# One-core hybrid decoder trunk on Trainium2: retention's weight differences on VectorE, the second norm in token layout, and GpSimd holding two groups of tiles

## The reference

```python
z = rmsnorm(h, norm_mix)
u, q, k, v, g, gate_a, gate_b = split(z @ w_in)
y_a = s5_branch(u, ...)                      # diagonal state space, GELU, GLU
y_b = retention_branch(q, k, v, g)           # 4 heads, chunks of 128, rotary, norm, silu(g)
merged = sigmoid(gate_a) * (y_a @ w_proj_ssm) + sigmoid(gate_b) * (y_b @ w_proj_ret)
h = h + merged @ w_out
z = rmsnorm(h, norm_mlp)
h = h + square(relu(z @ w_up)) @ w_down
return rmsnorm(h, norm_final)
```

## Time and profile before

| | |
|---|---|
| median of 3 runs | 1639.86 us (1639.55 to 1641.78) |
| the profiled execution: time / span | 1641.72 / 1639.9 us |
| busy: PE / DVE / POOL / ACT | 1557.7 / 741.6 / 474.5 / 285.1 us |
| granted TensorE clock, mean | 0.981 of full |

### The profile page before, as it was taken

One profiled execution on the slowest core, in us unless ns is written; L12 is line 12 of the kernel. 1 busy time (PEld: TensorE's weight loads), 2 busy tenths in 40 slices (PEclk: granted clock), 3 DMA queues, 4 the chain that ended last, 5 costly groups with the idle time before them and its releaser, 6 DMA issues.

```text
span 1639.9 us, 20796 instructions
## 1 busy us (share of the span) xinstructions
PE 1557.7 (95%) x7608; PEld 1304.7 (80%) x7608; DVE 741.6 (45%) x1610; ACT 285.1 (17%) x583; POOL 474.5 (29%) x267
## 2 busy tenths in 40 slices
PE   5996999999999999889999999999999999999996
PEld 4785788789888888777888888888888888888884
DVE  6797655551554546366624722323222222222225
ACT  4110111210222222132102410202010101001013
POOL 1331142333131313312333305142333324150601
PEclk9997999999999999999999999999999999999998
DMA  5342343354110101102441102011111102020202
GB/s 170 109 122 75 88 124 108 110 190 144 40 52 26 51 26 49 53 8 88 168 180 52 50 2 77 26 54 49 51 51 47 55 26 77 13 90 0 90 0 102
DMA packets 94210, 118.64 MB, mean 72 GB/s; under 512 B 24528, under 2 KB 58448, under 8 KB 94160
## 3 DMA queue, kind: packets, MB, share of 16 engines
q1 hardware_dynamic: 62416, 78.49, 14.8%
q10 hardware_dynamic: 31744, 39.48, 7.6%
HBM read 96.05 MB, written 20.97 MB: 71 GB/s over the span
## 4 chain that ended last, share of the span: by engine, by line
PE 84%; DVE 9%; SPq 2%; ACT 1%; issue 1%; ACTq 1%; DMA 1%; POOL 0%; DVEq 0%
PE acc L483 26%; PE acc L484 26%; PE acc L485 26%; SPq L343 1%; DVE tb L1507 1%; PE aux L721 1%; PE aux L727 1%; DVE rsn L1623 1%; DMA stage<-in_w_in 1%; PE aux L730 1%; PE aux L614 1%; DVE kvk L1626 1%; PE aux L620 1%; ACTq L951 1%; DVE y_raw L1529 0%
## 5 line engine op out<-in xcount | busy, mean ns | idle before, releaser
L422 POOL CAST w_hi<-stage 128x1024 fp32r<-128x1024 f32 x130 | 146.2, 1125 | 1068.9 <-PE acc L485 1028.4
L426 POOL TENSOR_TENSOR w_lo<-stage,w_hi 128x1024 fp32r<-128x1024 f32 x130 | 323.6, 2489 | 16.5 <-DVE x_in L1241 6.1
L483 PE MATMUL acc<-m_hi,w_hi 128*128 128x512 f32 x512 | 199.3, 389 | 0.0
L485 PE MATMUL acc<-m_hi,w_lo 128*128 128x512 f32 x512 | 199.2, 389 | 0.0
L484 PE MATMUL acc<-m_lo,w_hi 128*128 128x512 f32 x512 | 199.2, 389 | 0.0
L483 PE MATMUL acc<-w_hi,hid_hi 128*128 128x512 f32 x512 | 199.2, 389 | 0.0
L484 PE MATMUL acc<-w_lo,hid_hi 128*128 128x512 f32 x512 | 199.2, 389 | 0.0
L485 PE MATMUL acc<-w_hi,hid_lo 128*128 128x512 f32 x512 | 199.2, 389 | 0.0
L483 PE MATMUL acc<-z_hi,w_hi 128*128 128x512 f32 x448 | 179.4, 400 | 15.5 <-DVE z_lo L1208 10.8
L483 PE MATMUL acc<-w_hi,z_hi 128*128 128x256 f32 (+1 forms) x512 | 192.0, 375 | 0.0
L1764 DVE TENSOR_TENSOR h_res<-h_res,acc 128x512 f32<-128x512 f32 x128 | 87.9, 687 | 228.9 <-PE acc L485 228.9
(11 more groups left out here) (251 smaller groups left out, 2260.8 us busy)
## 6 DMA issues: line engine op xcount, KB each, us to landing
stage<-in_w_up SPq DMA_DIRECT2D x32, 512.0 KB, 3.6
stage<-in_w_down SPq DMA_DIRECT2D x32, 512.0 KB, 3.2
stage<-in_w_in SPq DMA_DIRECT2D x28, 512.0 KB, 3.7
gate_dram<-gate_t ACTq DMA_DIRECT2D x32, 256.0 KB, 2.0
x_in<-in_x SPq DMA_DIRECT2D x8, 512.0 KB, 8.9
stage<-in_w_in SPq DMA_DIRECT2D x32, 128.0 KB, 2.4
stage<-in_w_in SPq DMA_DIRECT2D x16, 256.0 KB, 3.0
gb_t<-gate_dram ACTq DMA_DIRECT2D x16, 256.0 KB, 2.7
```

The lines of the kernel that those rows point to most:

```text
L422: nc.gpsimd.tensor_copy(dst_hi, stage[:, s, :]).then_inc(hi_pool, 1)
L426: nc.gpsimd.tensor_tensor(dst_lo, stage[:, s, :], dst_hi.bitcast(F32), ALU.subtract)\
L483: nc.tensor.matmul(out, s_hi, m_hi_, start=first, stop=False)
L485: return nc.tensor.matmul(out, s_lo, m_hi_, start=False, stop=last)
```

## The change

The change has three parts. (1) For retention's 24 tiles and the first four of the ret projection GpSimd makes only the cast (`cast`); the difference is made by VectorE (`weight_lo`), at places written into its program: two in P_A, four between the first g blocks, then in each head two behind `decay` in steps 2 and 3 (`next_lo`; in the last head four, in steps 2 to 5) and four in steps 8 and 9 (`qkv_lo`). Behind its four casts for the ret projection GpSimd waits for all of `z_lo` before it goes on. (2) The second norm's scale and weight are applied by VectorE in one instruction, in token layout, before the transposes, with `norm_mlp` loaded as a row for all partitions and two buffers `zb`; the blocks are turned one chunk later, the last two behind the first and the second product of the MLP. `zb` and `nmlp` lie where `hid_lo` lies later. (3) In the MLP loop GpSimd waits for the last `zb` before the first down tile.

```diff
+            with ExitStack() as q:
+                hid_lo = sb("hid_lo", [P, FB // P, SEQ], F32R, q)
+            nmlp = sb("nmlp", [P, D], F32, r)
+            sb("hid_gap", [P, D], F32, r)
+            zb = sb("zb", [P, 2, D], F32, r)
...
         @block.gpsimd
+            def cast(ready, count, s, slot, u0, freed=None):
+                if freed is not None:
+                    pool.wait_ge(out_ready, freed)
+                pool.wait_ge(ready, count)
+                pool.sem_inc(tick_pool, 1)
+                dst_hi = w_hi[:, slot, u0:u0 + 2, :].rearrange("p k c -> p (k c)")
+                nc.gpsimd.tensor_copy(dst_hi, stage[:, s, :]).then_inc(hi_pool, 1)
...
             with pool.Fori(0, HEADS) as h:
                 for i in range(2):
                     n = LD_RET + i
-                    split(raw[n % 2], h * 16 + 16 * (LD_RET // 2 + 1), n % 2, GR_RET % 2, 2 * i, h * 6 + (n + 1),
-                          freed=h * 16 + (OUT_RET - 8) if i == 0 else None)
+                    cast(raw[n % 2], h * 16 + 16 * (LD_RET // 2 + 1), n % 2, GR_RET % 2, 2 * i,
+                         freed=h * 16 + (OUT_RET - 8) if i == 0 else None)
...
+            for i in range(4):
+                n = LD_PB + i
+                cast(raw[n % 2], 16 * (g_slot + i // 2 + 1), n % 2, GR_PB % 2, 2 * i, freed=OUT_PB - 8 if i == 0 else None)
+            pool.wait_ge(lo_done, SP_YB + KT)
             for base, gr in ((LD_PB, GR_PB), (LD_OUT, GR_OUT)):
-                for j in range(2):
+                for j in range(1 if base == LD_PB else 0, 2):
...
             with pool.Fori(0, N_FB) as f:
                 for b in range(2):
+                    if b == 1:
+                        pool.wait_ge(z2_scaled, NCH)
...
         @block.tensor
-                    if j == 1 and c >= 1:
-                        turn_z2(c - 1)
+                    if j == 1 and c >= 2:
+                        turn_z2(c - 2)
...
-                        if first and n == OUT_MLP + 1:
-                            turn_z2(NCH - 1)
+                        if first and n in (OUT_MLP + 1, OUT_MLP + 2):
+                            turn_z2(NCH - 3 + n - OUT_MLP)
...
         @block.scalar
-            act.dma_start(nmlp[:], t["norm_mlp"].rearrange("a (k p) -> p (a k)", p=P), allow_slow_non_contiguous=True)\
-               .then_inc(nmlp_in, 16)
...
             for c in range(NCH):
                 act.dma_start(h_res[:, c, :], x_rows[:, c, :]).then_inc(xr_in[c], 16)
+            nmlp_row = t["norm_mlp"]
+            act.dma_start(nmlp[:], bass.AP(tensor=nmlp_row.tensor, offset=0, ap=[[0, P], [1, D]])).then_inc(nmlp_in, 16)
...
             for c in range(NCH):
                 act.wait_ge(out_free, OUT_OUT + NCH + c + 1)
                 if c >= 1:
-                    act.wait_ge(z2_turned, 2 * c)
-                nc.scalar.activation(zb[:], h_res[:, c, :], ACT.Square, accum_out=ss2[:, c:c + 1]).then_inc(h_ss, 1)
-                if c >= 1:
-                    hi_z2(c - 1)
-                act.wait_ge(h_rstd, c + 1)
-                nc.scalar.activation(zb[:], h_res[:, c, :], ACT.Copy, scale=rs2[:, c:c + 1]).then_inc(z2_scaled, 1)
+                    act.wait_ge(h_ss, c)
+                nc.scalar.activation(h_junk[:], h_res[:, c, :], ACT.Square, accum_out=ss2[:, c:c + 1]).then_inc(h_ss, 1)
+                if c >= 2:
+                    hi_z2(c - 2)
+            hi_z2(NCH - 2)
             hi_z2(NCH - 1)
...
         @block.vector
+            def weight_lo(n, slot, u0, done):
+                dve.wait_ge(hi_pool, done)
+                V.tensor_tensor(w_lo[:, slot, u0:u0 + 2, :].rearrange("p k c -> p (k c)"), stage[:, n % 2, :],
+                                w_hi[:, slot, u0:u0 + 2, :].rearrange("p k c -> p (k c)").bitcast(F32), ALU.subtract)\
+                 .then_inc(w_ready, 1)
...
+                if n in (9, 10):
+                    weight_lo(LD_RET + n - 9, GR_RET % 2, 2 * (n - 9), LD_RET + n - 9 + 1)
...
                     if s <= NCH:
                         decay(s - 1)
+                    if s in (2, 3) or (s in (4, 5) and not more):
+                        next_lo(h, s - 2)
                     if more and s >= NCH:
                         g_silu(h + 1, 2 * (s - NCH) + 1)
+                        qkv_lo(h + 1, 2 * (s - NCH))
+                        qkv_lo(h + 1, 2 * (s - NCH) + 1)
...
             for c in range(NCH):
                 g_silu(0, c)
+                if 2 <= c < 6:
+                    qkv_lo(0, c - 2)
...
             def norm_z2(c):
-                for b in range(2):
-                    n = 2 * c + b
-                    dve.wait_ge(z2_turned, n + 1)
-                    V.tensor_tensor(aux[:, n % 4, :].rearrange("p (k s) -> p k s", k=4),
-                                    aux[:, n % 4, :].rearrange("p (k s) -> p k s", k=4),
-                                    nmlp[:, 4 * b:4 * b + 4].unsqueeze(2).broadcast_to([P, 4, P]), ALU.mult)\
-                     .then_inc(z2_normed, 1)
+                if c >= 2:
+                    dve.wait_ge(z2_turned, 2 * (c - 1))
+                V.scalar_tensor_tensor(out=zb[:, c % 2, :], in0=h_res[:, c, :], scalar=rs2[:, c:c + 1], in1=nmlp[:],
+                                       op0=ALU.mult, op1=ALU.mult).then_inc(z2_scaled, 1)
```

More of the change, by code:

```diff
@@ L122, in build @@
             hid_hi = sb("hid_hi", [P, FB // P, SEQ], F32R, r)
-            hid_lo = sb("hid_lo", [P, FB // P, SEQ], F32R, r)
+            with ExitStack() as q:
[3 more added lines that the diff above has]
+            zb = sb("zb", [P, 2, D], F32, r)
         ctx.enter_context(nc.sbuf_tensor("region1", [P, 2 * KT * SEQ], F32))
@@ L210, in build @@
             m_lo = sb("m_lo", [P, KT, SEQ], F32R, r)
-            nmlp = sb("nmlp", [P, KT], F32, r)
             ss2 = sb("ss2", [P, NCH], F32, r)
@@ L216, in build @@
                 ma_t = sb("ma_t", [P, HALF], F32, q)
-            with ExitStack() as q:
-                zb = sb("zb", [P, D], F32, q)
             with ExitStack() as q:
@@ L295, in build @@
         h_ss = sem("h_ss")
-        h_rstd = sem("h_rstd")
         z2_scaled = sem("z2_scaled")
         z2_turned = sem("z2_turned")
-        z2_normed = sem("z2_normed")
         squared = sem("squared")
@@ L452, in _ @@
                     n = LD_RET + i
-                    split(raw[n % 2], h * 16 + 16 * (LD_RET // 2 + 1), n % 2, GR_RET % 2, 2 * i, h * 6 + (n + 1),
-                          freed=h * 16 + (OUT_RET - 8) if i == 0 else None)
+                    cast(raw[n % 2], h * 16 + 16 * (LD_RET // 2 + 1), n % 2, GR_RET % 2, 2 * i,
+                         freed=h * 16 + (OUT_RET - 8) if i == 0 else None)
                 for i in range(4):
                     n = LD_RET + 2 + i
-                    split(raw_qkv[n % 2], h * 96 + 48 * (i // 2 + 1), n % 2, (GR_RET + 1) % 2, 2 * i, h * 6 + (n + 1),
-                          freed=h * 16 + OUT_RET if i == 0 else None)
+                    cast(raw_qkv[n % 2], h * 96 + 48 * (i // 2 + 1), n % 2, (GR_RET + 1) % 2, 2 * i,
+                         freed=h * 16 + OUT_RET if i == 0 else None)
             g_slot = LD_RET // 2 + HEADS
+            for i in range(4):
+                n = LD_PB + i
+                cast(raw[n % 2], 16 * (g_slot + i // 2 + 1), n % 2, GR_PB % 2, 2 * i, freed=OUT_PB - 8 if i == 0 else None)
+            pool.wait_ge(lo_done, SP_YB + KT)
             for base, gr in ((LD_PB, GR_PB), (LD_OUT, GR_OUT)):
-                for j in range(2):
+                for j in range(1 if base == LD_PB else 0, 2):
                     for i in range(4):
@@ L801, in turn_z2 @@
                         k = 4 * b + q
-                        mm = nc.tensor.transpose(aux[:, n % 4, q * P:(q + 1) * P], zb[:, k * P:(k + 1) * P], ident[:])
+                        mm = nc.tensor.transpose(aux[:, n % 4, q * P:(q + 1) * P], zb[:, c % 2, k * P:(k + 1) * P],
+                                                 ident[:])
                     mm.then_inc(z2_turned, 1)
@@ L1151, in hi_z2 @@
                     n = 2 * c + b
-                    act.wait_ge(z2_normed, n + 1)
+                    act.wait_ge(z2_turned, n + 1)
                     hi_split(m_hi[:, 4 * b:4 * b + 4, c * P:(c + 1) * P],
@@ L1687, in head, with qkv_lo, next_lo @@
                         lo_split(z_lo[:, k, cols], yb_raw[:, k, cols], z_hi[:, k, cols])
+            def qkv_lo(h, i):
+                n = LD_RET + 2 + i
+                weight_lo(n, (GR_RET + 1) % 2, 2 * i, h * 6 + (n + 1))
+            def next_lo(h, i):
+                n = LD_RET + 6 + i
+                weight_lo(n, GR_RET % 2, 2 * i, h * 6 + (n + 1))
             for c in range(NCH):
                 g_silu(0, c)
+                if 2 <= c < 6:
+                    qkv_lo(0, c - 2)
             with dve.Fori(0, HEADS - 1) as h:
@@ L1738, in _ @@
                 add_h(OUT_OUT + NCH + c, c, 1).then_inc(out_free, 1)
-                if c >= 1:
-                    norm_z2(c - 1)
                 dve.wait_ge(h_ss, c + 1)
```

(9 more changed lines are left out.)

## The result

The changed kernel takes 1612.38 us (median of 4 runs, 1611.75 to 1614.25) against 1639.7 (4 runs, 1637.8 to 1641.78) for the kernel before on the same chip: ratio 0.9836, 95% interval 0.982 to 0.9851. The profiled execution took 1612.35 us around a span of 1610.6.

What follows compares the result with a forecast made beforehand. TensorE bounds the kernel, so only its waits and low clock can be won. Terms -14.7 - 7.2 - 5.9 + 0.3 = -27.5 us, off the median 1639.86, give 1612.4 us; range 1610.7 to 1616.6, with scatter 1609.5 to 1618.

Steps and rivals of the forecast that it cites:

- Term A: Ends of the three looped heads: waits for the last rotation (9.1 us) and low clock behind them (5.6) go, 14.7 us.
- Term B: Start of the last head: the 5.4 us wait for the first rotation and 1.8 of low clock go, 7.2 us.
- Term C: End of the last head: the wait for `z_lo` falls to 2.7 us, total gain 5.9 us.
- Term D: Held second four W_pb tiles: their splits meet DVE's merge, costing 0.3 us, bounds 0 and 1.5.
- bounds 0 and 1.4: Last head's end: possible gain if the remaining 2.7 us stop brings no low clock; no gain was counted.
- Another short wait for `z_lo` at 749.3 goes: Behind the first ret-projection quad: a further PE wait of 0.2 us disappears.
- What DVE pays: Retention: 28 differences of 1.16 us, 32 us of work, fit DVE's gaps and cost nothing.
- The closest place: Looped head's end: last norm's `yb` comes at 476.4, PE's turn at about 478, 1.6 us to spare.
- Second norm and down tiles: Second norm and MLP: token-layout scaling and POOL's later down-tile splits make nobody wait, zero.
- The first: Rival, heads' ends: casts and late differences still cost one PE stop per head, A gone, 1627.1 us; chance 0.08.
- The second: Rival, ten steps: differences ahead of rotations wait for POOL's cast and stop PE, 1661 us; chance 0.03.
- The third: Rival, late rotations: the port is not the cause or casts alone stretch as much, 1640 us; chance 0.03.

Runs made afterwards that it cites:

- the gated kernel: Kernel before, POOL still casts and subtracts every tile but waits at three places for rotations or the last difference of y: 1613.63 us, ratio 0.9828.
- the filler: Changed kernel plus two extra matmuls into the first ret-projection quad's bank, ahead of its wait: 1612.88 us, ratio 0.9831.
- the run without the hold: Changed kernel without GpSimd's wait for the last difference of y before splitting W_pb's second half: 1620.35 us, ratio 0.9877.
- the new order: Changed kernel with ScalarE and VectorE work reordered at the last head's end: 1611.42 us, again 1610.92; with one extra matmul 1609.12.
- the norm alone: Kernel before with only the second norm in token layout and the hold of GpSimd's first down tiles: 1639.2 us, ratio 0.9992.

## Why the prediction was right

It named the mechanism and its places, and the time is 1612.38 where 1612.4 was said. The two traces, cut at POOL's marks, give each term:

| term | predicted | measured between the traces |
|---|---|---|
| A, ends of three heads | -14.7 | -15.2 (4.7 + 5.9 + 4.6) |
| B, start of the last head | -7.2 | -7.5 (64.54 to 57.08 us) |
| C and D, its end | -5.6 | -5.8 (56.02 to 50.21 us) |
| ahead of and behind retention | 0 | -0.8 (0.4 and 0.4) |
| sum | -27.5 | -29.3 |

(B runs from POOL's last mark, 668.67 and 653.07, to DVE's last rotation, 733.21 and 710.15.)

*The hit to 0.1 us is luck in part.* Against the profiled execution before (1641.72) the sum should have given 1614.2, and it took 1612.35. Taking the sum off the median of three (1639.86) absorbed this: the 42 runs of the kernel before beside the experiments have a median of 1641.4.

*Term A.* Right in the chain and in the size. The rotation was to end at 466.7 and ended at 466.43; PE asked at 467.51, so 1.1 us to spare, where 1.2 was said. Undoing it alone costs 14.5 us by the medians, 12.6 in the three heads of its trace, since one head lost no clock. The 5.6 us for low clock are thus the part of A that another run may not repeat; 9.1 us of waits it repeats.

*Term B.* Right; the wait and its low clock are gone (5.4 and 1.8 said, 7.46 together). No run undid it by itself; the gated kernel, in which POOL keeps these splits but waits, is rid of it too.

*Term C.* The wait fell from 8.45 to 2.59 us (2.7 said), and undoing the hold brought 8.5 back. One step of it was wrong where it did no harm: "bounds 0 and 1.4" counted a clock that stays up as a gain of 1.4 us. The stop of 2.59 us did bring the low clock, as chosen, but the filler, and the trace in which the clock stayed up by itself, show that without it only 0.25 us is won (107.29 to 107.04 and 107.03): the second `z_lo` is next in line. "Another short wait for `z_lo` at 749.3 goes" missed that it was only covered.

*Term D.* The collision is there, its price is not. DVE's timeline of the merge (alone each takes 0.69):

```profile
737.08 2.00 DVE L1743 TENSOR_TENSOR gb_t<-gb_t,ma_t 128x512 f32<-128x512 f32 x1
...
740.16 2.84 DVE L1221 TENSOR_TENSOR m_lo<-gb_t,m_hi 128x512 fp32r<-128x512 f32 x1 [1.08 <-ACT m_hi L878]
```

PE's product of the next output came 0.1 us late at 743.66; PE was busy 20.0 of 20 us from 736 to 756. 0.3 was said, within bounds.

*What DVE pays.* 28 differences of 1.22 us, not 1.16, and nobody waited:

```profile
L1226 DVE TENSOR_TENSOR w_lo<-stage,w_hi x28: 1215/1217/1226, 367.7 to 693.3; 128x1024 fp32r<-128x1024 f32 x28
```

The closest place, the last norm's `yb`, came at 475.70 + 0.48 (476.4 said), PE's turn of it at 477.64: 1.5 us to spare (1.6 said).

*Second norm and down tiles.* Zero as said; alone they are 1639.2 us.

*Rivals.* The first (casts cost as much as before) did not come true, but its condition is real: with six casts instead of two PE waits 2.1 us a head. The chance of 0.08 was fair for 1.1 us of slack. The second did not come near: in none of its ten steps does DVE wait for POOL's cast (the 6.0 us for which it does wait, in six places, lie ahead of the first head and behind the heads' ends), 0.65 us or more of its gap of 1.87 is left ahead of the rotation, and the rotation still waits for ACT, not for the difference. The third falls with the result and with the gated kernel; what it says of casts is true of each single one, as the run with six shows, but the two that stay do not reach far enough.

## What to carry to other kernels

When a short VectorE instruction with two SBUF inputs shows several times its usual length, compare its end with the ends of GpSimd's instructions: if they match, first try to hold GpSimd back with one wait at that place; here three waits gave all that moving 28 subtractions gave, to 1.3 us. Count the slack that is left in GpSimd instructions, since each can hold up one VectorE instruction, casts as well. And ask of every stall or slow clock on the path what is due right behind it: a filler that kept the clock up won 0.25 us, in the new order none at all; what bound the place was the order of two other engines.

## What the runs showed of the hardware

- One VectorE instruction per GpSimd cast where casts stand back to back: six in a row stretched five `tensor_tensor` of two SBUF inputs to 1.25, 0.94, 1.06, 1.06 and 1.06 us. I had expected one or two to get through. Between a cast and the subtraction that waits for its result a second one did (0.21 us at 713.78, in the run without the hold).
- It works in both directions: GpSimd's subtraction took 3.36 us instead of 2.40 where VectorE's difference of 1.21 us had come first.
- A `scalar_tensor_tensor` with two SBUF inputs is held up too (2.06 instead of 1.28 us), one with an input in PSUM is not (0.47).
- The low clock behind a stop is not certain, and a shorter stop can bring it: behind 3.0 us it came in seven of nine looped heads (three traces: the kernel before, the norm alone, q, k and v back on POOL), behind the 2.59 us before the first quad in six of seven traces (all that have this stop but the one with q, k and v back on POOL), behind 2.1 us in all three heads with six casts, and behind 1.32 us in neither of two traces. Why one escapes stays open.
